# Gate and SiLU buffers in PSUM, six product banks, and one low part per pair moved from GpSimd to VectorE

## The reference

```python
h = h + mixed @ w_o                                   # "wo", 8 blocks of 128 output channels
gt, up = jnp.split(rms_norm(h, norm2) @ w_gate_up, 2, axis=-1)   # D_FF = 2816 = 22 * 128
h = h + (jax.nn.silu(gt) * up) @ w_down               # "down", 8 blocks of 128 output channels
return rms_norm(h, final_norm)[:, N_META:]
```

## Time and profile before

| what | us |
|---|---|
| median of three runs | 1080.32 |
| lowest and highest run | 1079.17, 1080.46 |
| profiled execution, its own time | 1080.42 |
| span of the profiled execution | 1078.6 |
| busy: TensorE | 1039.0 (96%) |
| busy: VectorE | 638.4 (59%) |
| busy: GpSimd | 499.2 (46%) |
| busy: ScalarE | 482.8 (45%) |

### The profile page before, as it was taken

How to read it: one execution, slowest core, us unless ns; L and a number is a source line. 1 busy time by engine, 2 the same in 40 slices (tenths; PEclk the granted TensorE clock), 3 DMA queues, 4 the chain that set the end, 5 groups by cost and what they waited for, 6 DMA issues and landing times.

```text
span 1078.6 us, 22661 instructions
## 1 busy us (share of the span) xinstructions
PE 1039.0 (96%) x9025; PEld 925.3 (86%) x9025; DVE 638.4 (59%) x1141; ACT 482.8 (45%) x1069; POOL 499.2 (46%) x424
## 2 busy tenths in 40 slices
PE   8999999999999999999999999889999999889996
PEld 8889899989999999878888888689898989768886
DVE  6575757575766767644111223889999999941102
ACT  7735353545454454534223325654444444552222
POOL 0154636363636364544455556533333333544553
PEclk9999999999999999999999999999999999999999
DMA  6222222221212222212522332232332323312312
GB/s 222 73 88 68 73 69 71 70 79 60 90 60 80 69 70 62 78 61 86 187 82 95 98 98 81 77 98 99 98 99 94 102 91 106 118 59 98 98 59 78
DMA packets 28825, 95.61 MB, mean 89 GB/s; under 512 B 2984, under 2 KB 5288, under 8 KB 28720
## 3 DMA queue, kind: packets, MB, share of 16 engines
q1 hardware_dynamic: 27520, 91.77, 25.8%
q10 hardware_dynamic: 1200, 2.38, 0.6%
HBM read 92.03 MB, written 2.11 MB: 87 GB/s over the span
## 4 chain that ended last, share of the span: by engine, by line
PE 76%; DVE 16%; issue 4%; ACT 3%; DMA 0%; POOL 0%; DVEq 0%; ACTq 0%; SPq 0%; POOLq 0%
PE bank L1344 75%; DVE pair_sums L1213 3%; DVE tg L876 3%; DVE w_lo L1216 2%; DVE c L1228 2%; ACT w_hi L511 2%; DVE f_full L876 1%; DVE w_raw L1213 1%; DVE cst L1213 1%; DVE f_lo L1272 0%; DMA h_in<-h_t 0%; PE bank L1544 0%; PE bank L1538 0%; POOL w_lo L413 0%; DVE og_lo L1192 0%
## 5 line engine op out<-in xcount | busy, mean ns | idle before, releaser
L413 POOL TENSOR_TENSOR w_lo<-w_raw,w_hi 128x512 fp32r<-128x512 f32 x214 | 290.6, 1373 | 369.9 <-ACT w_hi L511 369.8
L1344 PE MATMUL bank<-x_hi,w_hi 128*128 128x258 f32 (+2 forms) x896 | 247.9, 335 | 0.3 <-DVE w_lo L887 0.3
L1344 PE MATMUL bank<-x_hi,w_lo 128*128 128x258 f32 (+2 forms) x896 | 230.3, 315 | 0.0
L1344 PE MATMUL bank<-x_lo,w_hi 128*128 128x258 f32 (+2 forms) x896 | 228.1, 316 | 0.0
L511 ACT ACTIVATE w_hi<-w_raw 128x512 fp32r<-128x512 f32 x290 | 171.7, 618 | 71.9 <-PE bank L1344 71.5
L1344 PEld LDWEIGHTS bank<-x_hi,w_lo 128*128 128x128 f32 x896 | 147.5, 189 | 11.2
L1344 PEld LDWEIGHTS bank<-x_hi,w_hi 128*128 128x128 f32 x896 | 146.3, 189 | 12.3 <-DVE w_lo L887 0.7
L1344 PEld LDWEIGHTS bank<-x_lo,w_hi 128*128 128x128 f32 x896 | 146.5, 189 | 8.9
L1344 PE MATMUL bank<-og_hi,w_hi 128*128 128x256 f32 (+1 forms) x416 | 125.8, 302 | 16.9 <-DVE w_lo L1216 16.9
L1344 PE MATMUL bank<-xe,w_hi 128*128 128x256 f32 (+1 forms) x602 | 125.1, 297 | 7.2 <-POOL w_lo L413 2.9
L1344 PE MATMUL bank<-og_hi,w_lo 128*128 128x256 f32 (+1 forms) x416 | 123.8, 298 | 0.0
(11 more groups left out here) (304 smaller groups left out, 1832.0 us busy)
## 6 DMA issues: line engine op xcount, KB each, us to landing
w_raw<-w_stream SPq DMA_DIRECT2D x146, 512.0 KB, 3.4
cst<-w_stream SPq DMA_DIRECT2D x16, 512.0 KB, 3.4
h_in<-h_t SPq DMA_DIRECT2D x4, 528.0 KB, 7.1
h<-h_t ACTq DMA_DIRECT2D x1, 2048.0 KB, 11.5
h_in<-gc_dram SPq DMA_DIRECT2D x7, 264.0 KB, 3.0
out<-h SPq DMA_DIRECT2D x4, 256.0 KB, 2.9
out<-h SPq DMA_DIRECT2D x2, 384.0 KB, 2.6
cst<-consts SPq DMA_DIRECT2D x1, 512.0 KB, 8.5
```

The lines of the kernel that those rows point to most:

```text
L413: nc.gpsimd.tensor_tensor(low_weights(n)[:, at], raw_weights(n)[:, at], high_weights(n)[:, at].bitcast(f32), ALU.subtract).then_inc(wlo_re ...
L1344: return nc.tensor.matmul(o, w, x, start=start, stop=stop)
```

## The change

Five things are edited, all from the wo blocks on.

1. tg and sg become PSUM banks 6 and 7; products rotate over the six banks 1, 3, 4, 5, 0, 2; TensorE's waits for joins follow, and the sum for the second norm goes to the bank of sg, so no product waits for rs2.
2. The low part of weight operand s1 moves from GpSimd to VectorE for pairs 1 to 21 (`ON_POOL` keeps parts 3 and 6). u and c22 become one join of 128x512.
3. In the wo blocks ScalarE makes both high halves of block n+1 first, at step 0, ahead of the chores of block n-1; in the last wo block it makes the high parts 0 and 1 of the first pair there, and GpSimd their low parts. VectorE makes s1 and s2 of the first pair at the start of that block. The orders in the first pair are changed a little.
4. The down projection takes m = 0 and m = 1 together, k by k, in four banks in turn.
5. `f_split` and `f_low` have a new order: one instead of two of each per place in the last pair; ScalarE's last ten `f_split` come after the high weights of the third down block.

The diff, cut to its core:

```diff
-DOWN_ENDS = {MAIN + (FT * m + FT - 1) // 8 + 1: m for m in range(KT)}
+DOWN_ORDER = [(m, k) for k in range(FT) for m in range(2)] + [(m, k) for m in range(2, KT) for k in range(FT)]
+DOWN_ENDS = {}
+for M in range(KT):
+    DOWN_ENDS.setdefault(MAIN + DOWN_ORDER.index((M, FT - 1)) // 8 + 1, []).append(M)
-ON_POOL = [0] + [NP * m + i for m in range(FT) for i in (1, 3, 6)]
+ON_POOL = [0, 1] + [NP * m + i for m in range(FT) for i in (3, 6)]
-JOINS = ("v", "w", "c11", "u", "c22", "c12", "c21")
+JOINS = ("v", "w", "c11", "uc22", "c12", "c21")
...
-        tg = sb("tg", [128, T], f32, ffn_mem)
-        sg = sb("sg", [128, T], f32, ffn_mem)
+        tail_ln = sb("tail_ln", [128, T], f32, ffn_mem)
+        scaled = sb("scaled", [128, T], f32, ffn_mem)
...
+        vw_parts = parts_mem[:, QUARTER:3 * QUARTER].rearrange("p (a t) -> p a t", t=QUARTER)
...
         def product_out(p):
-            return bank[(p + 6) % 8][:, 0:QUARTER]
+            return bank[(1, 3, 4, 5, 0, 2)[p % 6]][:, 0:QUARTER]
+        tg, sg = dbank[2], dbank[3]
+        def down_bank(m):
+            return bank[(0, 2, 1, 3)[m % 4]]
...
+                    if q in (1, 2) and n == FFN - 1:
+                        part_low(q - 1)
...
-            for p in ON_POOL:
+            for p in ON_POOL[2:]:
                 part_low(p)
...
+                    if q == 0 and BLOCKS[n][0] == "wo":
+                        for half in range(2):
+                            if n < FFN - 1:
+                                split_weights(n + 1, half)
+                            else:
+                                part_high(half)
...
-                    if q in (1, 2) and 5 <= n + 1 < FFN and not weights_first:
+                    if q in (1, 2) and 5 <= n + 1 < FFN and not weights_first and BLOCKS[n][0] != "wo":
                         split_weights(n + 1, q - 1)
...
-            part_high(0)
-            part_high(1)
             part_high(2)
...
                     if m < FT - 1:
                         part_high(p + 7 + i)
                     else:
-                        f_split(2 * i)
-                        f_split(2 * i + 1)
                         split_weights(MAIN + i // 2, i % 2)
+                        f_split(i)
                 if m == 0:
                     act.wait_ge(h_sums, 1)
-                    inverse_root(rs2[:, :], dbank[1][:, :], 1.0 / D, 0).then_inc(rs2_ready, 1)
+                    inverse_root(rs2[:, :], dbank[3][:, :], 1.0 / D, 0).then_inc(rs2_ready, 1)
             split_weights(MAIN + 1, 1)
             silu_gate(FT - 1)
-            for k in range(6, FT):
+            for k in range(3, EARLY_F):
                 f_split(k)
             for n in range(MAIN, STREAM + 1):
                 for half in range(2):
                     if MAIN + 2 <= n + 1 < STREAM:
                         split_weights(n + 1, half)
+                if n == MAIN + 1:
+                    for k in range(EARLY_F, FT):
+                        f_split(k)
...
-                nc.vector.tensor_tensor(to, product_out(NP * m + product), part, ALU.add).then_inc(joined, 1)
+                x = product_out(NP * m + product)
+                if name == "uc22":
+                    x = x.unsqueeze(1).broadcast_to([128, 2, QUARTER])
+                nc.vector.tensor_tensor(to, x, part, ALU.add).then_inc(joined, 1)
...
                 if n == FFN - 1:
                     weight_sum(0, "s1")
+                    weight_sum(0, "s2")
...
                 if m:
                     dve.wait_ge(f_ready, m)
-                join(m, "u")
-                join(m, "c22")
+                join(m, "uc22")
                 if m < FT - 1:
                     weight_sum(m + 1, "s2")
                 else:
-                    f_low(2)
-                    f_low(3)
+                    f_low(1)
+                if m < FT - 1:
+                    part_low(p + 8)
                 join(m, "c12")
                 if m < FT - 1:
                     part_low(p + 9)
                 scaled_gate(m)
             join(FT - 1, "c21")
-            f_low(4)
-            f_low(5)
+            f_low(2)
             gate_up(FT - 1)
-            for k in range(6, FT):
+            for k in range(3, FT):
                 f_low(k)
...
-                    if p + i in (2, 4):
-                        pe.wait_ge(h1_ready, KT - 1 if i == 2 else KT)
-                    elif p + i == 6:
+                    if m == 0 and i in (4, 5):
+                        pe.wait_ge(h1_ready, KT - 5 + i)
+                    if m == 0 and i == 6:
                         pe.wait_ge(sqa_ready, KT)
-                        mm(dbank[1][:, :], ones, sqa[:, :]).then_inc(h_sums, 1)
-                    elif p + i == 7:
-                        pe.wait_ge(rs2_ready, 1)
-                    elif m and i == 1:
-                        pe.wait_ge(part_copied, m)
-                    elif m and i:
-                        pe.wait_ge(joined, join_number(m - 1, ("w", "v", "c11", "c22", "c12")[i - 2]))
-                    elif m >= 2:
-                        pe.wait_ge(joined, join_number(m - 2, "c21"))
+                        mm(dbank[3][:, :], ones, sqa[:, :]).then_inc(h_sums, 1)
+                    if i == 6:
+                        pe.wait_ge(part_copied, m + 1)
+                    elif m:
+                        pe.wait_ge(joined, join_number(m - 1, ("w", "v", "c11", "uc22", "c12", "c21")[i]))
                     part_product(p + i, name, x_waits.get(i, {}))
             for d in range(DOWN):
                 n = MAIN + d
                 for i in range(8):
-                    m, k = divmod(8 * d + i, FT)
+                    m, k = DOWN_ORDER[8 * d + i]
...
-                    ins = products([big[m % 2][0][:, :]], n, i, [f_high(k)], [f_lo[:, k, :]], k == 0, k == FT - 1)
+                    ins = products([down_bank(m)[:, :]], n, i, [f_high(k)], [f_lo[:, k, :]], k == 0, k == FT - 1)
```

More of the change, by code:

```diff
@@ L488, in _ @@
                         split_weights(n + 1, half)
[L489 to L497 removed]
+                for m in DOWN_ENDS.get(n, []):
+                    if m == KT - 1:
+                        continue
+                    pool.wait_ge(h2_squared, m + 1)
+                    if m == 0:
+                        nc.gpsimd.tensor_copy(sqa_down[:, :], sqt_down[:, 0, :]).then_inc(sqf_ready, 1)
+                    else:
+                        pool.wait_ge(sqf_ready, m)
+                        nc.gpsimd.tensor_tensor(sqa_down[:, :], sqa_down[:, :], sqt_down[:, m % 2, :],
+                                                ALU.add).then_inc(sqf_ready, 1)
             pool.wait_ge(h2_scaled, KT - 1)
@@ L848, in _ @@
                         split_weights(n + 1, half)
+                if n == MAIN + 1:
+                    for k in range(EARLY_F, FT):
+                        f_split(k)
                 if n in EXP_LN_FROM:
                     nc.scalar.preload_act_table_set("natural_log_exp_and_others")
-                if n in DOWN_ENDS and DOWN_ENDS[n] < KT - 1:
-                    m = DOWN_ENDS[n]
+                for m in DOWN_ENDS.get(n, []):
+                    if m == KT - 1:
+                        continue
                     act.wait_ge(h2_ready, m + 1)
@@ L1263, in _ @@
             x_sum(KT - 1, "t3")
+            weight_sum(0, "s3")
             x_low(KT - 1, "t2")
@@ L1308, in _ @@
             join(FT - 1, "c21")
-            f_low(4)
-            f_low(5)
+            f_low(2)
             gate_up(FT - 1)
-            for k in range(6, FT):
+            for k in range(3, FT):
                 f_low(k)
             for n in range(MAIN, STREAM + 1):
-                if n in DOWN_ENDS and DOWN_ENDS[n] < KT - 1:
-                    m = DOWN_ENDS[n]
-                    if FT * (m + 1) % 8 == 0:
+                for m in DOWN_ENDS.get(n, []):
+                    if m == KT - 1:
+                        continue
+                    if DOWN_ORDER.index((m, FT - 1)) % 8 == 7:
                         dve.wait_ge(block_done, split_number(n))
                     else:
-                        dve.wait_ge(down_done, m + 1 - sum(FT * (i + 1) % 8 == 0 for i in range(m)))
+                        dve.wait_ge(down_done, m + 1 - sum(DOWN_ORDER.index((i, FT - 1)) % 8 == 7 for i in range(m)))
                     if m:
                         dve.wait_ge(h2_ready, m)
-                    link(mult(sg[:, :], big[m % 2][0][:, :], rs2[:, :]))
-                    nc.vector.tensor_tensor(h1[:, m, :], h1[:, m, :], sg[:, :], ALU.subtract).then_inc(h2_ready, 1)
+                    link(mult(scaled[:, :], down_bank(m)[:, :], rs2[:, :]))
+                    nc.vector.tensor_tensor(h1[:, m, :], h1[:, m, :], scaled[:, :], ALU.subtract).then_inc(h2_ready, 1)
             dve.wait_ge(h2_scaled, KT - 1)
@@ L1329, in _ @@
                     dve.wait_ge(h2_ready, KT - 1)
-                link(mult(sg[:, half], big[(KT - 1) % 2][i][:, 0:T // 2], rs2[:, half]))
```

(6 more changed lines are left out.)

41 lines of the change are left out of this document (16 added, 25 removed).

## The result

The changed kernel takes 1052.18 us (median of four runs, 1051.34 to 1056.89), the kernel before 1080.31; the ratio is 0.9751 [0.9721, 0.978]. The forecast was 1052.6. The profiled execution took 1052.21 us with a span of 1050.4, against 1080.42 and 1078.6.

What follows compares the result with a forecast made beforehand. VectorE's period was taken to bound the loop, with TensorE's waits in the fill and at down's start the rest. 1080.4 - 19.1 (loop) - 7.6 (fill) - 1.0 (down) = 1052.7, forecast 1052.6 us; range 1043.5 to 1062.

Steps and rivals of the forecast that it cites:

- The loop: In the 22 pairs, VectorE's period falls from 10.853 to 9.85 us: -19.1 us over 19 periods.
- the sum: For the loop, VectorE's period per pair: 10.853 - 1.11 + 0.51 - 0.45 + 0.09 - 0.06 = 9.83 us.
- the estimate of 1055.1: In the loop, PSUM reads cost tg and gate_up 0.065 us more each, 2.6 us over twenty pairs.
- The fill: Ahead of the steady loop, at most 9.7 us of stalls and low clock go, 2.1 return: net -7.6 us.
- New stalls that I expect: 2.1: In the fill: 0.9 us in product 2 for t2, 0.3 at product 6, 0.9 at products 10 and 11.
- the fill gives little: Rival: crowded wo blocks delay the last block's chain, +5 us, 1058 us; chance 0.11.
- Down: Down projection: new loss 0.4 + 5.0 + 1.7 = 7.1 us against 8.1 before, -1.0 us.
- I take the first, the same kind of row: Before the third down block: f_low's gapless row keeps GpSimd out until its end; TensorE stalls 5.0 us.
- the two readings: In down, GpSimd waits out the whole f_low row, -1.0 us, or gets in during it, -7.7 us.
- GpSimd gets its turn: Rival: in down, GpSimd gets in during the f_low row, -7.7 us there, 1045.9 us; chance 0.25.
- The slower rival, collisions at full price: Loop: each of GpSimd's two parts makes VectorE wait 1.29 us, period 11.90, 1093.6 us; chance 0.03.

Runs made afterwards that it cites:

- The two undoing runs: Changed kernel with the low part of s1 back on GpSimd, 1058.92 us; changed kernel with tg and sg back in SBUF, 1067.99 us.
- the third run: Changed kernel with ScalarE's high halves behind the chores again in the wo blocks, parts 0 and 1 still early: 1052.4 us, ratio 0.9753.
- runs one, two, four, five and six: Changed kernel with, in order: s1's low part on GpSimd, 1058.92; tg, sg in SBUF, 1067.99; down m by m, 1054.84; nothing changed, ratio 0.9762; f_low gaps, 1050.03 us.
- the last run: Changed kernel with f_low gaps and VectorE making low parts 0, 1, 3, plus GpSimd's last three sums of squares cut to 2 columns: 1047.01 us.
- the four kernels with that gap: Changed kernel with f_low gaps, 1050.03 us; plus reordered fill, 1050.51; or plus low parts 0, 1, 3 on VectorE, 1050.06; the latter with sums of squares cut, 1047.01.
- the seventh run: Changed kernel with first-pair s1 and s2 moved behind block 6's step and chain, ScalarE's high part 1 behind its block 6 scaling: ratio 0.9769.
- the fourth run: Changed kernel with the down projection running m by m again: 1054.84 us, ratio 0.9769.
- the fifth run: Changed kernel repeated unchanged with five more timed runs: 1050.94 to 1060.78 us, ratio 0.9762.

## Why the prediction was right, and where its sum was not

**The loop: right, item by item.** tg at 0.69 (taken 0.60 as a distance, 806.76 to 807.36 is that), s2 at 0.68, s3 waiting for GpSimd's part (1.18 us as a distance, 807.36 to 808.54; 1.11 in the sum), the low part of s1 half hidden. tg to tg, the nineteen periods from 718.34 to 905.69 us give 9.86 against the 9.85 taken. VectorE alone needs 9.82 (the first eight of them), where the sum has 9.83. The two undoing runs price the items in the kernel's time: 0.37 us per pair for the moved part, 0.53 for PSUM. The bound is another than the sum had it, though: not VectorE at 9.83 beside TensorE at 9.80, but TensorE, at 9.89. Its matmuls stand 0.1178 us apart and not 0.1167; in the profile of the third run, where they stand 0.1167 apart, the period is 9.81. Writing into PSUM cost nothing (0.42 for the join, 0.69 for tg), so the 120 fixed cycles that the Trainium skill (VectorE: DVE Perf Modes, section on the TRN2 errata) gives to PSUM against 58, and the estimate of 1055.1 from them, do not show here.

**The fill: the mechanism right up to the first product, then mis-sized.** Up to the first product the change brought 2.9 us, which is the three stops 0.79, 0.82 and 1.21. From there to product 4 of pair 1 it was 23.82 us and is 23.36: -0.5, where -4.5 stood in the sum; so the first down matmul is at 914.69 and not at about 910. The step that failed is "New stalls that I expect: 2.1". They are 1.87 + 0.79 + 1.02 = 3.7. The 0.79 for t2 and the 1.02 at product 11 stood in the sum, with 0.9 each; the 1.87 for low part 2, which VectorE makes only behind h1 of the last block, did not. And behind the first two the clock goes to 1.2 GHz for 6.8 us, 2.7 us of work, where the sum had no low clock left at all: 6.4 instead of 2.1. How long the low clock lasts is not fixed by the program: of the five other profiled executions with these stops (runs one, two, four, five and six) one has 6.8 us, three have 3.4 and one has none. The cause named in the rival "the fill gives little" is the one: the crowded chain. h1 of the last block starts at 692.28, 3.0 us after the block's end; in the last run, where s1 no longer waits, it is 2.05 us, and these are VectorE's chain of block 6. Low part 2 (1.16) and t2 (1.50) wait for GpSimd behind h1 again. The last run shows that the traffic of GpSimd's sums of squares costs 3.0 us, with what the clock adds; moving VectorE's own work about, or taking GpSimd's over, gave nothing. From the first product to product 4 of pair 1 these runs have 23.66, 22.81 and 22.97 us, the first profile and those five 22.53 to 23.36, and the last run 19.97. The wo reordering by itself is worth nothing measurable (third run).

**Down: the step that failed is "I take the first, the same kind of row".** The stop before the third block was forecast at 5.0 us by the reading that a row of f_low without a gap keeps GpSimd out. In the profiled execution GpSimd got in at 921.98 at once, and was kept out only at 929.66, for 3.67 us, which cost 1.04. In the profile of the repeated run it went as forecast: 9.13 us, a stop of 4.43 and the clock behind it. So the two readings, and the earlier trace rows, were not two rules of which one is valid, but two outcomes of one contest. Which one comes can't be read from the trace of before: the two profiles of the changed kernel have their request at the same point of the row (3.50 us in), with opposite ends. Nor is it the point within an f_low: 0.19 us into one, the request got in with the low part of s1 on GpSimd (928.84) and with the wo chores first (919.94), and was shut out with tg in SBUF (931.90). The Trainium skill (SBUF — State Buffer, Who interferes with whom) has the shared ports granted to whoever issues first, for a whole instruction; the request at 921.98 agrees with it, those at 929.66 in the same execution, at 924.53 in the repeated run and at 931.90 with tg in SBUF don't. What decides between the outcomes stays open. That starting VectorE's operations 0.80 us apart instead of 0.60 ends it is shown as far as the four kernels with that gap go: in their profiles no GpSimd part of the row takes over 1.9 us, and none of their 18 executions is above 1050.9. Of 18 executions without it (the changed kernel, its repeat, the third and the seventh run) seven are at 1054 to 1061.

**The forecast's time.** With -3.4, -18.6 and -6.2 it came to 1052.2 instead of 1052.6; an error of +4.2 in the fill and one of -5.2 in down cancel, with 0.5 left over in the loop. That the total came so near is luck. In the one profiled execution of the changed kernel where down goes as forecast the time is 1060.78, still inside the range; 1056.89 and 1056.96 would fit the same, but have no trace. The rival "GpSimd gets its turn" was given 0.25 and is what the profiled execution of 1052.21 does in front of the third block; its 1045.9 missed by 4.2 in the fill, 1.5 in down (1.04 of it the stop in front of the fourth block) and 0.5 in the loop. The slower rival, collisions at full price, has its measurement in the loop: s3 takes 1.25 and s1 0.93 us, instead of 0.68, so a part costs 0.57 and 0.25 us and not 1.29.

## What to carry to other kernels

A row of back-to-back operations on VectorE can keep a GpSimd operation that shares its memory ports waiting until the row ends, or not, within one and the same program; where something late hangs on that operation, put a short wait between VectorE's, if VectorE has slack. In a fill, count collisions between the two engines like work: moving them about or exchanging them for work of the same size gave nothing here, only less traffic did. And check a right total by its parts: here two errors of 4 and 5 us cancelled.

## What was not expected of the hardware

TensorE's 128x256 matmuls come at one of several fixed paces, at a granted clock of 1.00 throughout. In the kernel before it is 0.1178 us per matmul from 715 to about 755 us and 0.1167 behind it; in the first profile of the changed kernel 0.1167 at first and 0.1178 from about 722 us to the end of the loop (84 x 0.1178 = 9.89); with the gap the change comes at about 800 us; in the repeated run it is 0.1200 from about 725 us on, 10.08 us for 84. The third run (wo blocks) has 0.1167 up to the end; its profiled execution took 1050.53 us. Over 20 pairs, 0.1167 to 0.1200 is 5.5 us, more than most edits studied here, and it could be why the times of the fifth run do not fall into two groups; that is not shown, as only one of them has a trace. The 512-column matmuls of the down projection show nothing of it, 0.2333 us in every profile. What sets the pace was not found.

The clock went to 1.2 GHz behind stops: 6.8 us behind one of 4.43 and one of 4.70, 3.4 us behind one of 2.89 in the kernel before, 3.4 us behind one of 1.71 in the fourth run, 6.8 or 3.4 us behind the pairs of stops of the fill, none behind the same pair in the repeated run (1.90 and 1.38), none behind a stop of 1.04 or one of 0.42 followed by 1.21. So the stops alone do not tell whether it falls. What it costs is in the rows: with 5.79 us busy at 0.425 instead of 0.2333 us per 512-column matmul, 2.6 us.
